# Scores ahead of the turned probabilities, in a two-block transformer kernel on one core

## The chip, the core and the metric

The kernel runs on one NeuronCore of a Trainium2 chip. TensorE (PE) multiplies matrices: a weight load puts a stationary operand into the array (PEld in the trace), a matmul streams the moving operand past it into PSUM, eight banks of 512 floats per partition. VectorE (DVE) and ScalarE (ACT) work on SBUF and PSUM, GpSimd (POOL) does a few small operations and DMA issues, SyncE (SP) issues the stream of weights. Each engine works through its own queue in order; between engines only semaphores order the work. The metric is the device time of one execution in microseconds, the median of three runs.

## The reference

Two blocks of two layers each on a sequence of 256 tokens, width 1024, float32. In the first block every layer is a half FFN, a mixing of four attention branches, and another half FFN. The four branches (MLA, sliding window, NSA and differential attention) are all softmax attention over 256 keys:

```python
s = jnp.einsum('bhqd,bhkd->bhqk', qb, k).astype(jnp.float32) * scale
s = s + rel_bias(table, qpos, kpos)[:, None]
s = jnp.where(kpos[None, :] <= qpos[:, None], s, NEG)
p = jax.nn.softmax(s, -1)
return jnp.einsum('bhqk,bhkd->bhqd', a.astype(v.dtype), v)
```

Each branch is projected and gated: `merged + sigmoid(u @ w_gate) * (y @ w_branch)`. The first layer of the second block has dilated attention: 16 heads, three groups of dilation 1, 4 and 16, a softmax in each group and one over the groups. The second layer has retention instead, which the change leaves alone.

## The kernel before

All weights come as one stream of slots (3072 floats per partition) through a ring of four. Most slots are split on the chip into a high part (ACT, L1456, `ring_hi`) and a low part (DVE, L1778, `ring_lo`), and PE multiplies high by high, high by low and low by high (`uT,ring_hi` and `uT,ring_lo` in the trace, all at L829, the helper `mm`). PE says by the semaphore `ring_used` that a slot has been read. The helper `mm` carries that signal: a finished slot adds to `pending`, and the next call of `mm` sends it. Transposes and the values of dilated attention don't go through `mm`.

**Attention of the first block.** Two heads make a pair. There are 20 pairs per layer (0 to 3 MLA, 4 to 7 sliding window, 8 to 11 differential, 12 to 19 NSA) and 22 steps. Before the change, step t does on PE, in this order:

- `turn(l, t)` (L1101): transposes of the probabilities of pair t-1, 128x128 each, six of them (three for a differential pair). It waits for `probs_normed`, which DVE signals.
- `scores(l, t)`: queries times keys of pair t into PSUM banks 0 and 1. It waits for `biased`, by which DVE says that the scores of pair t-1 have been read.
- two projections or merges (24 matmuls or more with `uT,ring_hi`), each waiting for its PSUM bank, which DVE empties (`qkT`, L2074, or `mlaT_all`, L2334).
- `values(l, t-1)`: probabilities times values for pair t-1.

DVE in step t: `bias_max` (L2256, L2258, adds the bias and takes the maximum), a low split (L1778), an addition of a branch (L2332, L2334), `normalise` (from L2272), a gate. ACT in step t: a high split (L1456), `copy_pT` (L1675, the transposed probabilities out of PSUM), a gate (L1680), then `exps` (L1663, L1664). DVE's and ACT's orders are written out and the same after the change.

The array is used in three cuts. The trace writes them as rows*columns: transposes and projections are 128*128, the scores of all pairs but MLA have a contraction of 64 and run in two halves by rows, 64*128, and the values of all pairs but differential write 64 columns each, 128*64.

**Dilated attention.** 17 steps for 16 score blocks (`NS2` = 16). Step s does `dilated_turn(s-1)` (L1295, eight transposes), `dilated_scores(s)` (12 matmuls, L829, `qkT`), four projections for the next pair of heads (`dilated_pieces`, none from step 14 on), and `dilated_values(s-1)` (L1309). DVE: `dilated`, bias and maximum at L1937, then low splits and copies of projections (L1912), then reciprocal and scaling (L1956, L1957). ACT: copies of the transposes (L1544), exps (L1549), copies of projections and high splits. At the end of an odd step ACT stands before a high split which waits for `ring_used` of the slot that the last projection of that step has read. The signal is still `pending` then, and is sent by the first matmul of the next scores.

Of the kernel before, what the change touches and what calls it, by code (L numbers as in the profile page):

```python
# [166 lines left out]
def build(nc, stream, x_rows, norm_gT_2, gains_2, table_2, pick_2, ret_const, decay, norm_gT, mla_gT, sinks, posT, lam, subln, table_1, consts, flip_dram, pick_1, out):  # L167

    ctx = ExitStack()
    with ctx:  # L170
# [276 lines left out]
        NS2 = HEADS_2  # L447
# [92 lines left out]
        PAIRS = NU // 2  # L540
# [37 lines left out]
        def unit_q(u):  # L578
            kind, n = u["kind"], u["head"]
            if kind == "mla":  # L580
                return mlaT[:, n, 0:SEQ]
            if kind == "diff":
                return qkT[64 * u["map"]:64 * u["map"] + 64, T_DQ + n, :]
            base = T_SQ if kind == "swa" else T_NQ
            return qkT[64 * (n // 4):64 * (n // 4) + 64, base + n % 4, :]

        def unit_k(u):
            kind, n = u["kind"], u["head"]
            if kind == "mla":
                return mlaT[:, n, SEQ:2 * SEQ]  # L590
            if kind == "diff":
                return qkT[64 * u["map"]:64 * u["map"] + 64, T_DK + n, :]
            tile = {"swa": T_SK, "sel": T_KS, "win": T_KW}[kind]
            return qkT[64 * (n // 4):64 * (n // 4) + 64, tile, :]
# [21 lines left out]
        def piece(l, what, n):  # L616

            return l * PIECES_LAYER + PIECE_INDEX[what, n]
# [16 lines left out]
        def piece_copied(n):  # L635

            mine = sum(ON_ACT[:n + 1])
            return (piece_act_out, mine) if ON_ACT[n] else (piece_dve_out, n + 1 - mine)
# [7 lines left out]
        def tile_at(i):  # L646

            return 9 + i if i < 12 else None

        def merge_at(i):  # L650

            return i - 12 if i >= 12 else None
# [143 lines left out]
        def _(pe):  # L796
# [31 lines left out]
            def mm(out_, lhsT, rhs, start, stop, **kw):  # L828
                m = pe.matmul(out_, lhsT, rhs, start=start, stop=stop, **kw)  # L829
                if pending[0]:  # L830
                    m.then_inc(ring_used, pending[0])
                    pending[0] = 0
                return m
# [232 lines left out]
            def scores(l, t):  # L1066
                a, two = l * NU + 2 * t, UNITS[2 * t:2 * t + 2]
                if a >= 2:
                    pe.wait_ge(biased, a)
                if t == 0:  # L1070
                    pe.wait_ge(*piece_copied(piece(l, "head", 6)))
                    pe.wait_ge(*piece_copied(piece(l, "head", 7)))
                if t in (4, 8, 12):
                    pe.wait_ge(*piece_copied(piece(l, "tile", {4: 6, 8: 20, 12: 20}[t])))
                for cols, q_cols, k_cols in ((slice(0, P), slice(0, P), slice(0, P)),
                                             (slice(P, 3 * P), slice(P, SEQ), slice(0, SEQ))):
                    for j, u in enumerate(two):
                        m = mm(ps[:, j, cols], unit_q(u)[:, q_cols], unit_k(u)[:, k_cols], True, True)
                        if cols.start:
                            m.then_inc(scores_ready, 1)  # L1080

            def turn(l, t):
                if t in (2, 3):
                    pe.wait_ge(cmp_taken, 2 * l + t - 1)
                if t == 4:
                    pe.wait_ge(cmp_kv_out, l + 1)
                if t == 5:
                    pe.wait_ge(cmp_vB, l + 1)
                if t == 6:
                    pe.wait_ge(cmp_shifted, l + 1)  # L1090
                if t == 9:
                    pe.wait_ge(cmp_pT, l + 1)
                if t == 15:
                    pe.wait_ge(branch_in, COPIES_LAYER * l + COPIES_OF_BRANCH[3])
                for j in range(jobs(t - 1)):
                    n = jobs_before(l, t - 1) + j
                    pe.wait_ge(probs_normed, n + 1)
                    if l or t > 1:
                        pe.wait_ge(pT_ready, jobs_before(l, t - 1))
                    for b in range(3):  # L1100
                        last = pe.transpose(ps[:, 2 + j, b * P:(b + 1) * P], probs_sb[:, j, b * P:(b + 1) * P], ident)  # L1101
                    last.then_inc(probs_turned, 1)
# [43 lines left out]

            def attention(l):
                for t in range(STEPS):
                    if 1 <= t <= PAIRS:
                        turn(l, t)  # L1150
                    if t < PAIRS:
                        scores(l, t)
                    for i in (2 * t, 2 * t + 1):
                        if tile_at(i) is not None:
                            tile(l, tile_at(i))
                        else:
                            merge(l, merge_at(i))
                        compress(l, t, i % 2)
                        if i == 28:
                            turn_diff(l, t)  # L1160
                    if 1 <= t <= PAIRS:
                        values(l, t - 1)
# [103 lines left out]
            def dilated_scores(s):  # L1266


                hp, qt = s // 2, s % 2
                b = hp % 2  # L1270
                if qt == 0:
                    pe.wait_ge(*piece_copied(PIECES_DIL + 8 * hp + 5))
                if s:
                    pe.wait_ge(biased_2_ready, 2 * s)
                for g in range(N_GROUPS):
                    for j in range(2):
                        r = slice(64 * j, 64 * j + 64)
                        q = qkD[r, b, 2 * g, qt * P:(qt + 1) * P]
                        k = qkD[r, b, 2 * g + 1, :] if g == 0 else qkD[r, b, 2 * g + 1, qt * P:(qt + 1) * P]
                        o = ps[:, j, 0:256] if g == 0 else ps[:, j, 128 * (g + 1):128 * (g + 2)]  # L1280
                        m = mm(o, q, k, True, True)
                        if g == N_GROUPS - 1:
                            m.then_inc(scores_2, 1)
# [30 lines left out]
            def dilated(c0, p):  # L1314
                dilated_pieces(c0, 0, range(8), p)
                for s in range(NS2 + 1):
                    if s:
                        dilated_turn(s - 1)
                    if s < NS2:
                        dilated_scores(s)  # L1320
                    hp = s // 2 + 1
                    if hp < 8:
                        dilated_pieces(c0, hp, range(4 * (s % 2), 4 * (s % 2) + 4), p)
                    if s:
                        dilated_values(s - 1)
                pe.wait_ge(pT_2_ready, 2 * NS2)
                out_project(c0 + 24, lambda k, tt: mT_2[:, k, tt * P:(tt + 1) * P], KD, p, (stored_2, 1))
# [1372 lines left out]
```

## Time and profile before

| what | value |
|---|---|
| median of three runs | 2904.51 us (2904.24 to 2905.25) |
| the profiled execution | 2901.78 us |
| its span, first to last instruction | 2900.0 us |
| PE, DVE, ACT, POOL busy | 96%, 62%, 46%, 4% |
| attention of the first block, layer 0 | about 304 to 531 us |
| attention of the first block, layer 1 | about 1047 to 1274 us |
| dilated attention | about 1747 to 1990 us |

A row of a timeline gives start and length in microseconds, the engine, the line, the operation and its operands, and in brackets how long the engine had been idle before it and who released it. A row of the waits gives engine and line, who was waited for, the sum, the number and the longest.

### The profile page before, as it was taken

Reading aid. Unit: us, or ns where it says so; the run is one execution under the profiler, and the core shown is the slowest. Engines: PE = TensorE matmul, PEld = TensorE weight load, DVE = VectorE, ACT = ScalarE, POOL = GpSimd, SP = SyncE. Lnnn points to the kernel's source line nnn. Section 1 sums busy time; section 2 is a strip of 40 time slices with the busy share of each in tenths; the row PEclk is TensorE's granted clock in tenths of the full one; section 3 lists DMA queues with packets and bytes.
Section 4 is the critical chain, followed back from the end, with each engine's and each line's share of the span. In section 5 each row is a group of like instructions: output and inputs, shape, how many; then the busy total and the mean of one; then the engine's idle time right before and its main releaser. Section 6 shows DMA issues by size and latency. Waiting matters only on the chain.

```text
span 2900.0 us, 41202 instructions
## 1 busy us (share of the span) xinstructions
PE 2798.5 (96%) x16526; PEld 2384.0 (82%) x16526; DVE 1795.7 (62%) x2753; ACT 1328.2 (46%) x1913; POOL 104.0 (4%) x135
## 2 busy tenths in 40 slices
PE   7999999999999999999999999998999998999998
PEld 6888988688888888877878879996887887986787
DVE  5666566366766656645667665554667666652665
ACT  4553444155554444424554544443545554451444
POOL 1000000000000000001002001110000000000000
PEclk9999999999999999999999999999999999999999
DMA  6554333345454543345555445443454554434443
GB/s 239 189 199 153 139 147 131 139 167 195 174 184 184 196 153 132 131 152 208 194 186 183 182 165 171 168 156 128 174 192 161 187 195 153 174 133 151 165 183 123
DMA packets 49042, 488.40 MB, mean 168 GB/s; under 512 B 6480, under 2 KB 6576, under 8 KB 10520
## 3 DMA queue, kind: packets, MB, share of 16 engines
q1 hardware_dynamic: 43192, 470.44, 44.1%
q0 software_dynamic: 5728, 16.25, 1.9%
q8 instruction: 87, 1.43, 0.2%
q14 instruction: 35, 0.29, 0.0%
HBM read 485.47 MB, written 1.19 MB: 168 GB/s over the span
## 4 chain that ended last, share of the span: by engine, by line
PE 87%; DVE 6%; ACT 3%; issue 2%; DMA 1%; POOL 0%; DVEq 0%; ACTq 0%; POOLq 0%
PE ps L829 67%; PE ps L887 16%; DVE ring_lo L1778 2%; ACT ring_hi L1456 2%; PE ps L1101 1%; PE ps L845 1%; DMA norm_g<-norm_gT_dram 1%; PE ps L1295 1%; PE ps L1309 1%; PE ps L1206 0%; DVE xn L1888 0%; DVE uT L1802 0%; PE ps L898 0%; PE ps L953 0%; DVE h L1897 0%
## 5 line engine op out<-in xcount | busy, mean ns | idle before, releaser
L829 PE MATMUL ps<-uT,ring_hi 128*128 128x512 f32 (+1 forms) x5536 | 1516.1, 345 | 30.6 <-DVE mlaT_all L2334 10.9
L829 PE MATMUL ps<-uT,ring_lo 128*128 128x256 f32 x4176 | 1176.4, 282 | 0.0
L829 PEld LDWEIGHTS ps<-uT,ring_hi 128*128 128x128 f32 x5536 | 955.4, 190 | 185.8 <-DVE ring_lo L1778 18.2
L829 PEld LDWEIGHTS ps<-uT,ring_lo 128*128 128x128 f32 x4176 | 794.4, 190 | 6.2
L1854 DVE TENSOR_TENSOR ring_lo<-ring,ring_hi 128x2048 fp32r<-128x2048 f32 x167 | 382.8, 2292 | 230.8 <-ACT ring_hi L1498 230.8
L1778 DVE TENSOR_TENSOR ring_lo<-ring,ring_hi 128x3072 fp32r<-128x3072 f32 (+1 forms) x100 | 297.0, 2971 | 172.7 <-ACT ring_hi L1456 172.6
L1456 ACT ACTIVATE ring_hi<-ring 128x3072 fp32r<-128x3072 f32 (+1 forms) x100 | 246.0, 2460 | 320.1 <-PE ps L829 227.6
L1498 ACT ACTIVATE ring_hi<-ring 128x2048 fp32r<-128x2048 f32 x174 | 330.8, 1901 | 0.0
L887 PE MATMUL ps<-ring_hi,hid_hi 128*128 128x512 f32 x704 | 276.8, 393 | 9.8 <-DVE hid_lo L1849 9.8
L887 PE MATMUL ps<-ring_lo,hid_hi 128*128 128x512 f32 x704 | 276.0, 392 | 0.0
L887 PE MATMUL ps<-ring_hi,hid_lo 128*128 128x512 f32 x704 | 274.0, 389 | 0.0
L829 PE MATMUL ps<-ring_hi,uT 128*128 128x384 f32 (+1 forms) x1024 | 258.9, 332 | 3.4 <-DVE ring_lo L1778 1.8
L1488 ACT ACTIVATE work_all<-ps 128x512 f32<-128x512 f32 x176 | 105.3, 598 | 327.3 <-PE ps L829 327.0
L1491 ACT ACTIVATE work_all<-work_all 128x256 f32<-128x256 f32 x176 | 73.7, 418 | 318.5 <-DVE work_all L1842 318.5
L1834 DVE TENSOR_TENSOR ring_lo<-ring,ring_hi 128x1024 fp32r<-128x1024 f32 x176 | 214.5, 1219 | 0.5 <-ACT ring_hi L1486 0.5
L829 PEld LDWEIGHTS ps<-ring_hi,uT 128*128 128x128 f32 x1024 | 183.5, 188 | 5.5 <-DVE ring_lo L1778 4.4
L1486 ACT ACTIVATE ring_hi<-ring 128x1024 fp32r<-128x1024 f32 x176 | 184.0, 1045 | 0.0
L829 PE MATMUL ps<-ring_lo,uT 128*128 128x384 f32 (+1 forms) x512 | 169.2, 330 | 0.0
L887 PEld LDWEIGHTS ps<-ring_hi,hid_hi 128*128 128x128 f32 x704 | 132.1, 188 | 43.9 <-DVE hid_lo L1849 13.1
L887 PEld LDWEIGHTS ps<-ring_hi,hid_lo 128*128 128x128 f32 x704 | 132.2, 188 | 29.1
L887 PEld LDWEIGHTS ps<-ring_lo,hid_hi 128*128 128x128 f32 x704 | 132.2, 188 | 21.0
L1839 DVE TENSOR_TENSOR work_all<-ps,work_all 128x512 f32<-128x512 f32 x176 | 121.4, 690 | 43.5 <-ACT work_all L1488 43.2
(274 smaller groups left out, 2493.3 us busy)
## 6 DMA issues: line engine op xcount, KB each, us to landing
ring<-stream_dram SPq DMA_DIRECT2D x299, 1536.0 KB, 6.3
mlaT_all<-bias_vectors POOLq DMA_DIRECT2D x32, 96.0 KB, 2.9
bias<-gains_dram POOLq DMA_DIRECT2D x5, 512.0 KB, 7.7
yR<-bias_vectors POOLq DMA_DIRECT2D x1, 2048.0 KB, 10.5
mlaT_all<-bias_vectors POOLq DMA_DIRECT2D x32, 64.0 KB, 3.3
row<-ret_const_dram POOLq DMA_DIRECT2D x1, 1280.0 KB, 5.8
h<-x_rows_dram POOLq DMA_DIRECT2D x2, 512.0 KB, 11.6
yR<-gains_dram POOLq DMA_DIRECT2D x2, 512.0 KB, 11.4
```

What stands on the lines that cost most here:

```text
L829: m = pe.matmul(out_, lhsT, rhs, start=start, stop=stop, **kw)
L845: last = pe.transpose(ps[:, banks[kp], j * SEQ + tt * P:j * SEQ + tt * P + P], h[:, tt, k * P:(k + 1) * P], ident)
L887: last = pe.matmul(ps[:, n, :], x, w[:, cols], start=False, stop=final and x is x_lo, skip_group_check=True)
L1456: act.activation(split_part(c, high(c)), split_part(c, ring[:, c % NS, :]), ACT.Copy)\
L1486: act.activation(high(c)[:, 2 * D:3 * D], ring[:, c % NS, 2 * D:3 * D], ACT.Copy).then_inc(down_hi, 1)
L1488: act.activation(gu_low, ps[:, 4 + 2 * (g % 2):6 + 2 * (g % 2), SEQ:2 * SEQ], ACT.Copy)\
L1491: act.activation(sil[:, g % 2, :], gu[:, g % 2, 0, :], ACT.Silu).then_inc(silu_ready, 1)
L1498: act.activation(high(c)[:, 0:2 * D], ring[:, c % NS, 0:2 * D], ACT.Copy).then_inc(hi_ready, 1)
L1778: dve.tensor_tensor(split_part(c, ring_lo[:, c % NS, :]), split_part(c, ring[:, c % NS, :]), split_part(c, high(c).bitcast(F32)), ALU.subt ...
L1834: dve.tensor_tensor(ring_lo[:, c % NS, 2 * D:3 * D], ring[:, c % NS, 2 * D:3 * D], high(c)[:, 2 * D:3 * D].bitcast(F32), ALU.subtract)
L1839: dve.tensor_tensor(gu[:, g % 2, :, :], ps[:, 4 + 2 * (g % 2):6 + 2 * (g % 2), 0:SEQ], gu_low, ALU.add).then_inc(gu_summed, 1)
L1854: dve.tensor_tensor(ring_lo[:, c % NS, 0:2 * D], ring[:, c % NS, 0:2 * D], high(c)[:, 0:2 * D].bitcast(F32), ALU.subtract).then_inc(lo_rea ...
```

## The change

In both loops the call for the scores is put in front of the call for the transposes. Nothing is added or removed, on no engine; DVE's, ACT's, POOL's and SP's orders stay as they are. A blank line that comes with it moves the line numbers behind it by one (L1295 and L1309 are L1296 and L1310 in the changed kernel).

```diff
@@ attention(l), first block @@
                 for t in range(STEPS):
+
+                    if t < PAIRS:
+                        scores(l, t)
                     if 1 <= t <= PAIRS:
                         turn(l, t)
-                    if t < PAIRS:
-                        scores(l, t)
@@ dilated(c0, p) @@
                 for s in range(NS2 + 1):
+                    if s < NS2:
+                        dilated_scores(s)
                     if s:
                         dilated_turn(s - 1)
-                    if s < NS2:
-                        dilated_scores(s)
```

PE in step 18 of the first block's attention, layer 0, before. `yR,ring` are the last matmuls of step 17's merge, `work_all,row` the values of pair 16, `cst,work_all` the transposes, `qkT` the scores, `uT` the next merge:

```order
L829 MATMUL ps<-yR,ring 128x256 x4
L829 MATMUL ps<-work_all,row 64x256 x2
L829 MATMUL ps<-work_all,row 64x128 x2
L1101 MATMUL ps<-cst,work_all 128x128 x6
L829 MATMUL ps<-qkT 128x128 x2
L829 MATMUL ps<-qkT 128x256 x2
L829 MATMUL ps<-uT,ring_hi 128x256 x2
L829 MATMUL ps<-uT,ring_lo 128x256
```

The same place in the changed kernel:

```order
L829 MATMUL ps<-yR,ring 128x256 x4
L829 MATMUL ps<-work_all,row 64x256 x2
L829 MATMUL ps<-work_all,row 64x128 x2
L829 MATMUL ps<-qkT 128x128 x2
L829 MATMUL ps<-qkT 128x256 x2
L1101 MATMUL ps<-cst,work_all 128x128 x6
L829 MATMUL ps<-uT,ring_hi 128x256 x2
L829 MATMUL ps<-uT,ring_lo 128x256
```

The six transposes have moved behind the four score matmuls, right ahead of the merge; values and scores now follow each other directly.

PE at the end of dilated attention, steps 14 to 16, before (`mlaT_all,work_all` are transposes, `work_all,row` values; the last rows are the output projection):

```order
L1309 MATMUL ps<-work_all,row 64x128 x8
L1295 MATMUL ps<-mlaT_all,work_all 128x128 x8
L829 MATMUL ps<-qkT 128x256 x2
L829 MATMUL ps<-qkT 128x128 x4
L1309 MATMUL ps<-work_all,row 64x128 x8
L1295 MATMUL ps<-mlaT_all,work_all 128x128 x8
L829 MATMUL ps<-qkT 128x256 x2
L829 MATMUL ps<-qkT 128x128 x4
L1309 MATMUL ps<-work_all,row 64x128 x8
L1295 MATMUL ps<-mlaT_all,work_all 128x128 x8
L1309 MATMUL ps<-work_all,row 64x128 x8
L829 MATMUL ps<-ring,yR 128x512 x28
```

And in the changed kernel:

```order
L1310 MATMUL ps<-work_all,row 64x128 x8
L829 MATMUL ps<-qkT 128x256 x2
L829 MATMUL ps<-qkT 128x128 x4
L1296 MATMUL ps<-mlaT_all,work_all 128x128 x8
L1310 MATMUL ps<-work_all,row 64x128 x8
L829 MATMUL ps<-qkT 128x256 x2
L829 MATMUL ps<-qkT 128x128 x4
L1296 MATMUL ps<-mlaT_all,work_all 128x128 x8
L1310 MATMUL ps<-work_all,row 64x128 x8
L1296 MATMUL ps<-mlaT_all,work_all 128x128 x8
L1310 MATMUL ps<-work_all,row 64x128 x8
L829 MATMUL ps<-ring,yR 128x512 x28
```

The last scores (second group of `qkT`) no longer stand behind the transposes of step 14's probabilities.

## Rows read from the trace of the kernel before

**Rows 1.** The page's first part: busy time, share of the span, instructions.

```profile
PE 2798.5 (96%) x16526; PEld 2384.0 (82%) x16526; DVE 1795.7 (62%) x2753; ACT 1328.2 (46%) x1913; POOL 104.0 (4%) x135
```

**Rows 2.** The page's chain that ended last, by engine.

```profile
PE 87%; DVE 6%; ACT 3%; issue 2%; DMA 1%; POOL 0%; DVEq 0%; ACTq 0%; POOLq 0%
```

**Rows 3.** PE's waits in attention, layer 0, 330 to 530 us: sum, times, longest.

```profile
PE ps L829 <- DVE mlaT_all L2334: 5.4, 4, 2.7
```

**Rows 4.** PE's waits in attention, layer 1, 1070 to 1271 us.

```profile
PE ps L829 <- DVE mlaT_all L2334: 5.5, 5, 2.7
```

**Rows 5.** PE's waits in dilated attention, 1720 to 1992 us.

```profile
PE ps L829 <- DVE qkT L1912: 4.0, 7, 2.0
PE ps L1295 <- DVE work_all L1957: 3.6, 4, 1.6
```

**Rows 6.** Timeline of PE, step 18 of layer 0: transposes, scores, merge.

```profile
502.18 0.87 PE L1101 MATMUL ps<-cst,work_all 128*128 128x128 f32 x6
502.99 0.93 PE L829 MATMUL ps<-qkT 64*128 64x128 f32 x8
503.84 0.50 PE L829 MATMUL ps<-uT,ring_hi 128*128 128x256 f32 x2
504.18 0.28 PE L829 MATMUL ps<-uT,ring_lo 128*128 128x256 f32 x1
504.30 0.40 PE L829 MATMUL ps<-uT,ring_hi 128*128 128x256 f32 x2
```

**Rows 7.** Timeline of PE, step 10 of layer 0 (differential, values uncut): transposes, scores.

```profile
407.09 0.49 PE L1101 MATMUL ps<-cst,work_all 128*128 128x128 f32 x3
407.51 0.93 PE L829 MATMUL ps<-qkT 64*128 64x128 f32 x8
```

**Rows 8.** Timeline of all engines, step 18 of layer 0.

```profile
502.12 2.77 ACT L1456 ACTIVATE ring_hi<-ring 128x3072 fp32r<-128x3072 f32 x1 [3.47 <-PE ps L829]
503.94 0.29 DVE L2256 CUSTOM_DVE_ANT_0 xn<-ps,bias 128x128 f32<-128x128 f32 x1 [2.03 <-PE ps L829]
505.50 3.35 DVE L1778 TENSOR_TENSOR ring_lo<-ring,ring_hi 128x3072 fp32r<-128x3072 f32 x1
509.69 0.50 PE L829 MATMUL ps<-uT,ring_hi 128*128 128x256 f32 x2 [0.99 <-DVE mlaT_all L2334]
```

**Rows 9.** Timeline of all engines, step 2 of dilated attention, an even step.

```profile
1779.83 1.09 PE L1295 MATMUL ps<-mlaT_all,work_all 128*128 128x128 f32 x8
1780.85 1.15 PE L829 MATMUL ps<-qkT 64*128 64x256 f32 x12
1781.64 2.77 ACT L1456 ACTIVATE ring_hi<-ring 128x3072 fp32r<-128x3072 f32 x1 [2.15 <-PE ps L829]
1784.45 3.36 DVE L1778 TENSOR_TENSOR ring_lo<-ring,ring_hi 128x3072 fp32r<-128x3072 f32 x1 [0.54 <-ACT ring_hi L1456]
1787.67 0.28 PE L829 MATMUL ps<-uT,ring_lo 128*128 128x256 f32 x1
1788.29 0.48 PE L829 MATMUL ps<-uT,ring_hi 128*128 128x256 f32 x2 [0.34 <-DVE qkT L1912]
```

**Rows 10.** Timeline of all engines, steps 15 and 16 of dilated attention.

```profile
1981.44 0.65 PE L1295 MATMUL ps<-mlaT_all,work_all 128*128 128x128 f32 x4 [1.62 <-DVE work_all L1957]
1982.91 1.15 PE L829 MATMUL ps<-qkT 64*128 64x256 f32 x12
1983.02 0.60 ACT L1544 ACTIVATE work_all<-ps 128x512 f32<-128x512 f32 x1 [0.29 <-PE ps L1295]
1984.09 0.69 DVE L1937 CUSTOM_DVE_ANT_1 xn<-ps,mlaT_all 128x512 f32<-128x512 f32 x1 [1.82 <-PE ps L829]
1985.02 0.72 ACT L1549 ACTIVATE work_all<-xn,small 128x512 f32<-128x512 f32 x1 [1.40 <-DVE small L1941]
1988.81 1.98 PE L1309 MATMUL ps<-work_all,row 128*64 128x128 f32 x16 [0.69 <-ACT work_all L1544]
```

**Rows 11.** Window: length; busy PE, PEld, DVE, ACT, POOL; granted clock; DMA.

```profile
1988.50:1994.80 6.30, 6.00 (x21) 3.41 (x22) 1.06 (x6) 4.17 (x6) 0.00 (x0) 0.50 0.00 0
```

## The prediction

> **What bounds the kernel now.** I read the page first: PE is busy for 2798.5 of 2900.0 us [rows 1], and the chain that ended last runs over PE for 87% of the span [rows 2]. So the time is PE's own pace plus the few stretches in which it waits. DVE at 62% and ACT at 46% matter only where they release PE. The reader should see from this that a change of order can pay in two ways alone: PE's instructions follow each other faster, or a wait of PE gets shorter.
>
> Next came PE's waits in the three stretches that the change touches. Attention of the first block has 5.4 us in layer 0 and 5.5 us in layer 1, all on DVE's addition of a branch [rows 3, 4]. None stands on L1101: the transposes never wait there, and the scores don't either. Dilated attention has 4.0 us on DVE's copy of a projection, seven times, and 3.6 us in front of its transposes, four times [rows 5]. Those are all the waits that can be won. Last I read the timelines to see what holds these waits, and how PE gets from one kind of matmul to the next.
>
> **Part 1: fewer changes of the array's cut.** The same transposes take 1.09 us for eight [rows 9] and 0.65 us for four [rows 10], each with a change of cut ahead of it, so one more transpose is 0.44 / 4 = 0.11 us. In step 10, where the values ahead are uncut and the transposes follow without a change, three last 0.42 us from their start to the scores' start [rows 7], against 3 x 0.11 = 0.33: 0.09 us go at the change to 64*128. In step 18 six last 502.99 - 502.18 = 0.81 us against 0.66 [rows 6]: 0.15, so a group behind a change also loses some 0.06 on its second instruction. Behind the scores, the merge's first two matmuls take 0.34 us where two at the later pitch of 0.12 (504.18 to 504.30) would take 0.24 [rows 6]: 0.10 more. A change from scores to projections thus costs 0.09 + 0.10, about 0.2 us.
>
> Now count. With values cut 128*64 ahead (as in the last of rows 10), a step before goes values, transposes, scores, projection: 128*64, 128*128, 64*128, 128*128, three changes. After it goes values, scores, transposes, projection: 128*64, 64*128, 128*128, 128*128, two changes, because transposes and projections share a cut. The one into the projection goes: 0.2 us. The other two stay, with an order that the trace doesn't have (narrow values straight into row-cut scores). I take it at the price of the others; it could be free (0.2 us better) or cost two changes (0.2 us worse, and the gain is nil).
>
> In the first block these are steps 4 to 9 and 14 to 19, since values at the end of step t-1 are those of pair t-2. MLA steps 2 and 3 keep one change (their scores are uncut) and gain nothing. Steps 10 to 13 have uncut values ahead, two changes before and two after, and win only 0.10 - 0.06, say 0.05. Steps 14, 18 and 19 end in a wait of PE on DVE that swallows what PE gains in front of it, and step 13 runs into the first of them, so none of the four counts here. That leaves 9 steps x 0.2 + 3 x 0.05 = 1.95 us per layer, 3.9 for two. Dilated attention: steps 2 to 13, 12 x 0.2 = 2.4; from step 14 on there are no projections behind. Part 1 is 6.3 us. Its bounds are 0 and, with the direct change free in the same 30 steps, 12.3.
>
> The Trainium skill, "TensorEngine Tiling (Array Packing)", Key Properties, says of the direct change, which no row shows: "Changing tiling mode (not just tile) drains the TensorE". By it narrow values into row-cut scores is one drain like the others, and part 1 would be the 6.3 us; it gives no price, so this decides nothing above.
>
> **Part 2: steps 18 and 19 of the first block.** PE waits 0.99 us at 509.69 [rows 8], and the longest wait is 2.7 us, in each layer [rows 3, 4]; that one is the same place in step 19. The chain: scores end, DVE takes bias and maximum at 503.94 (it had been idle for 2.03 us waiting for PE), then a low split of 3.35 us at 505.50, then the addition that frees PE's bank. In the new order the scores begin where the transposes began, 0.81 us sooner [rows 6], and so does DVE at 503.94. But the low split also needs ACT's high split, which ends at 502.12 + 2.77 = 504.89 [rows 8] and hangs on the values, not on the scores. So the low split starts at about 504.95 rather than 505.50: 0.55 us. PE's wait falls from 0.99 to about 0.45 and stays a wait, so the whole 0.55 is won. Four such places (two steps, two layers): 2.2 us. Bounds 0 and 4 x 0.81 = 3.2.
>
> What do the moved transposes hold up? `copy_pT` stands ahead of the exps on ACT. In step 18 ACT is busy with the high split until 504.89 anyway, and the new transposes are done by then (502.18 + 0.85 for the scores + 0.81). So it costs nothing there.
>
> **Part 3: even steps of dilated attention.** Here the signal is what counts. ACT's high split at 1781.64 had been waiting for PE: for `ring_used`, pending since the end of the step before, and sent by the first score matmul, which starts at 1780.85 [rows 9]. In the new order that matmul starts where the transposes did, at 1779.83: 1.02 us sooner. ACT then starts at 1780.62, ends at 1783.39; DVE's bias and maximum come 1.02 sooner too, so its low split starts at about 1783.45 rather than 1784.45 and the copy of the projection behind it is 1.0 us earlier. PE waited for that copy: 1788.29 - 1787.67 = 0.62 against a pitch of 0.12, so 0.50 us lost [rows 9]. PE arrives 0.2 us sooner (part 1), the copy 1.0: the wait is gone with 0.3 to spare. The seven waits of rows 5 sum to 4.0; the longest, 2.0, is at step 0, which has no transposes and doesn't change. Six remain, 0.34 each in that view, 0.50 by the starts: 3.0 us. Bounds 0 and 6 x 0.62 = 3.7.
>
> **Part 4: the tail.** In steps 14 to 16 nothing covers the softmax. Before, PE does the transposes of step 14 (1981.44, and four more behind), then scores 15 at 1982.91; DVE's maximum starts at 1984.09, the exp at 1985.02 [rows 10]. In the new order scores 15 run right behind values 13, inside PE's wait of 1.62 us, so bias and maximum of 15 follow DVE's scaling of 14 at once. What is late next is ACT: its copies of step 14's transposes stand ahead of the exp and end at 1983.02 + 0.60 = 1983.62. The exp then starts at 1983.62 rather than 1985.02: 1.4 us, and all behind it, up to the last values at 1988.81, comes that much sooner. If the exps of step 14 also start sooner, it is up to 0.4 more. Bounds 0.3 (half the maximum hidden, transposes late) and 1.8.
>
> **Sum.** 6.3 + 2.2 + 3.0 + 1.4 = 12.9 us. The profiled execution took 2901.78 us, so it would be 2888.9. The median is 2904.51, 2.7 above that execution, and I take the saving off the median: 2891.6 us. Bounds of the four together: 0.3 and 21, neither end likely.
>
> **The rivals.**
> - *Waits go, changes of cut don't* (chance 0.16). Narrow values into row-cut scores costs two changes. For it: the trace has no such pair. Against it: every change that it has costs about the same. Then part 1 is nil, 6.6 us are won, 2897.9.
> - *The half-speed stretch behind the tail goes as well* (0.12). From 1988.50 to 1994.80 the granted clock was 0.50, the 1.2 GHz level, [rows 11], after PE had waited in front of the transposes of steps 15 and 16 [rows 5, 10]. In the new order those waits are shorter. At 2.4 GHz the same 6.3 us are worth 3.15: 2888.4. Against it: waits of over a microsecond remain in front of the last transposes. The Trainium skill, "TensorE: Matmul & The Clock Gate", HAM oscillation, says that gaps of the array bring the lower clock back; by it this rival is right if the rest of the gaps is short enough, which the rows before don't tell. The opposite, one more such stretch elsewhere, costs the same.
> - *Only faster following, no wait shortened* (0.06). DVE's and ACT's starts depend on something else than the scores and the signal. Against it: both were idle and released by PE [rows 8, 9]. Part 1 alone: 2898.2.
> - *Slower: the direct change is dear* (0.03). Values in column halves followed by scores in row halves occur 38 times in the new order (12 steps x 2 layers, 14 in dilated attention). If PE let the one finish wholly before it loads for the other, at 0.9 us each (as long as the scores' 0.85 us block in rows 6) instead of 0.2, it is 26.6 us lost against 12.9 won: 2918. It turns slower from 0.54 us each on. Nothing in the trace comes near this without a wait.
>
> That the change does nothing isn't a rival: PE's order moves in every step.
>
> **How the numbers follow.** My forecast has 0.60, the rivals 0.37, and 0.03 is for what I don't see. From no change this kernel's measurement can tell about 0.2%, 5.8 us. Forecast, the second and nearly all of the first and third rival are faster than that. Of the first rival (6.6) and the third (6.3) a third could fall within it, with a little from others: same 0.08. Slower 0.04, faster 0.88. The range goes from 2885 (direct change partly free, or a half-speed stretch gone) to 2898 (the first and third rival).
>
> **What would show each step.** Part 1: in step 4 to 9 the projection's first two matmuls take 0.24 us rather than 0.34, with no gap between transposes and projection. Part 2: PE's waits on L2334 about 1.1 us less per layer, so 4.3 and 4.4. Part 3: waits on L1912 once, not seven times. Part 4: scores 15 ahead of the transposes of step 14, and from those transposes' start (1981.44 before) to the last values' (1988.81) about 6 us rather than 7.4. I am wrong if PE starts to wait for the transposes' input in steps with projections, if ACT's copies of the transposes delay the exps beyond where they began before, or if dilated attention and the first block's attention together are not 10 us shorter.

## The result, and the profile after

The changed kernel takes 2884.89 us (median of four runs, 2883.84 to 2888.06) against 2904.38 us before (four runs, 2902.84 to 2905.25). The ratio is 0.9935, 95% interval 0.9918 to 0.9953: 19 us less, 14 to 24 by the interval. The forecast was 2891.6 us, 2885 to 2898. A second set of runs of the same kernel (experiment 9) gave 20 us. So the direction held, nearly all its mechanisms did, and the size was a third too small: the time lies at the lower end of the range (2884.89 against 2885), and 3 us of what brought it there were not in the forecast (see the clock below). The profiled executions give 2900.0 us of span before and 2882.4 after, 17.6 us, and that difference can be divided.

The page after, busy time and the chain by engine, to set beside [rows 1, 2]. PE is busy for 12 us less with as many instructions; that this comes from fewer changes of cut and less time at the lower clock is likely, but no run separates it. The other engines differ by 2 us at most:

```profile
PE 2786.3 (97%) x16526; PEld 2383.4 (83%) x16526; DVE 1796.6 (62%) x2753; ACT 1326.4 (46%) x1913; POOL 103.9 (4%) x135
PE 89%; DVE 5%; ACT 3%; issue 2%; DMA 1%; POOL 0%; DVEq 0%; ACTq 0%; POOLq 0%
```

PE's waits after, first block, layer 0 (330 to 530 us); layer 1 has 4.6 too. Before it was 5.4 and 5.5 [rows 3, 4]. The first row is the loader's, whose waits the prediction left out:

```profile
PEld ps L829 <- DVE mlaT_all L2335: 6.0, 5, 2.6
PE ps L829 <- DVE mlaT_all L2335: 4.6, 4, 2.3
```

PE's waits after, dilated attention (1715 to 1980 us). The copy of a projection is waited for once, not seven times, and the 3.6 us in front of the transposes [rows 5] have become 0.2. In their place stand 2.3 us in front of the values, where it was 0.7:

```profile
PE ps L1310 <- ACT work_all L1545: 2.3, 3, 0.8
PE ps L829 <- DVE qkT L1913: 2.0, 1, 2.0
PE ps L1296 <- DVE work_all L1958: 0.2, 1, 0.2
```

Step 18 of layer 0 after, PE; it answers to [rows 6]. Values, scores, transposes, merge. From the start of the first group behind the values to the third matmul of the merge it was 504.18 - 502.18 = 2.00 us, and is 501.11 - 499.30 = 1.81:

```profile
498.50 0.87 PE L829 MATMUL ps<-work_all,row 128*64 128x256 f32 x8
499.30 0.93 PE L829 MATMUL ps<-qkT 64*128 64x128 f32 x8
500.16 0.87 PE L1101 MATMUL ps<-cst,work_all 128*128 128x128 f32 x6
500.79 0.48 PE L829 MATMUL ps<-uT,ring_hi 128*128 128x256 f32 x2
501.11 0.28 PE L829 MATMUL ps<-uT,ring_lo 128*128 128x256 f32 x1
506.25 0.51 PE L829 MATMUL ps<-uT,ring_hi 128*128 128x256 f32 x2 [0.62 <-DVE mlaT_all L2335]
```

ACT and DVE in the same step, to set beside [rows 8]. The high split ends at 499.25 + 2.77 = 502.02, and the low split starts at 502.05: DVE no longer holds it up, ACT does. Its idle time in front of the maximum fell from 2.03 to 1.23 us:

```profile
499.25 2.77 ACT L1457 ACTIVATE ring_hi<-ring 128x3072 fp32r<-128x3072 f32 x1 [3.90 <-PE ps L829]
500.26 0.29 DVE L2257 CUSTOM_DVE_ANT_0 xn<-ps,bias 128x128 f32<-128x128 f32 x1 [1.23 <-PE ps L829]
502.05 3.36 DVE L1779 TENSOR_TENSOR ring_lo<-ring,ring_hi 128x3072 fp32r<-128x3072 f32 x1
505.77 0.43 DVE L2335 TENSOR_TENSOR mlaT_all<-mlaT_all,work_all 128x256 f32<-128x256 f32 x1
```

Step 2 of dilated attention after, to set beside [rows 9]. The high split starts 0.80 us behind the first score matmul, as before (1781.64 - 1780.85 = 0.79), but the scores now come first, so ACT's idle time is 1.13 instead of 2.15 us. The row before the last is the matmul that had waited 0.34 us; it follows the one at 1779.86 by 0.12:

```profile
1772.22 1.15 PE L829 MATMUL ps<-qkT 64*128 64x256 f32 x12
1773.02 2.78 ACT L1457 ACTIVATE ring_hi<-ring 128x3072 fp32r<-128x3072 f32 x1 [1.13 <-PE ps L829]
1773.30 1.09 PE L1296 MATMUL ps<-mlaT_all,work_all 128*128 128x128 f32 x8
1775.83 3.36 DVE L1779 TENSOR_TENSOR ring_lo<-ring,ring_hi 128x3072 fp32r<-128x3072 f32 x1 [0.55 <-ACT ring_hi L1457]
1779.10 0.42 DVE L1913 SCALAR_TENSOR_TENSOR qkT<-ps,r_row 128x256 f32<-128x256 f32 x1
1779.86 0.28 PE L829 MATMUL ps<-uT,ring_lo 128*128 128x256 f32 x1
1779.98 0.40 PE L829 MATMUL ps<-uT,ring_hi 128*128 128x256 f32 x2
1780.22 0.28 PE L829 MATMUL ps<-uT,ring_lo 128*128 128x256 f32 x1
```

The tail after, to set beside [rows 10]: scores 15 stand in PE's old wait, the eight transposes of step 14 run in one piece, ACT copies both halves in one piece and goes on to the exp. From those transposes to the last values it is 1973.49 - 1968.19 = 5.30 us; it was 1988.81 - 1981.44 = 7.37:

```profile
1967.12 1.15 PE L829 MATMUL ps<-qkT 64*128 64x256 f32 x12
1968.19 1.09 PE L1296 MATMUL ps<-mlaT_all,work_all 128*128 128x128 f32 x8
1968.29 0.69 DVE L1938 CUSTOM_DVE_ANT_1 xn<-ps,mlaT_all 128x512 f32<-128x512 f32 x1
1968.88 1.08 ACT L1545 ACTIVATE work_all<-ps 128x512 f32<-128x512 f32 x2 [1.45 <-PE ps L1296]
1969.86 0.72 ACT L1550 ACTIVATE work_all<-xn,small 128x512 f32<-128x512 f32 x1
1973.49 1.10 PE L1310 MATMUL ps<-work_all,row 128*64 128x128 f32 x16 [0.69 <-ACT work_all L1545]
```

The window of 6.30 us from the last values on, columns as in [rows 11], starting 0.3 us later in the work, at the values themselves. Before, the clock there was 0.50 and PE got through 21 matmuls; now it is 1.00, the 2.4 GHz level, and 29:

```profile
1973.49:1979.79 6.30, 6.30 (x29) 3.26 (x30) 2.21 (x7) 3.93 (x5) 0.00 (x0) 1.00 0.00 0
```

**Where the time went.** PE has the same matmuls in both kernels, so each can be matched with itself. The table gives how far PE's starts moved against the profile before, as differences over a stretch (minus is gained). Half-speed stretches that differ between the two stand in rows of their own.

| stretch | forecast | after |
|---|---|---|
| first block, layer 0 | -3.05 | -3.9 |
| first block, layer 1 | -3.05 | -4.1 |
| dilated attention, steps 2 to 13 | -5.4 | -5.8 |
| its tail, to the last values | -1.4 | -1.9 |
| the half-speed stretch behind the tail is gone | 0 | -3.0 |
| other half-speed stretches, start | 0 | +1.1 |
| sum | -12.9 | -17.6 |

So 15.7 us come from the order of the instructions. The rest is nearly all where PE ran at the lower clock: a stretch at 1517 us got shorter (-1.3), the one at 1715 cost 0.4 more, and one each appeared at 1749 and 2005 (+1.5, +0.8).

### The profile page after: what moved, and what is told of

The parts are those of the page before. It is cut to its first block, busy times and chain, and to the rows that moved or that the text cites. A ratio compares the mean times of both kernels' runs of the same rounds, so it can differ in the third digit from the quotient of the medians.

```text
span 2882.4 us, 41202 instructions
## 1 busy us (share of the span) xinstructions
PE 2786.3 (97%) x16526; PEld 2383.4 (83%) x16526; DVE 1796.6 (62%) x2753; ACT 1326.4 (46%) x1913; POOL 103.9 (4%) x135
## 4 chain that ended last, share of the span: by engine, by line
PE 89%; DVE 5%; ACT 3%; issue 2%; DMA 1%; POOL 0%; DVEq 0%; ACTq 0%; POOLq 0%
PE ps L829 68%; PE ps L887 16%; ACT ring_hi L1457 2%; DVE ring_lo L1779 1%; PE ps L845 1%; PE ps L1101 1%; DMA norm_g<-norm_gT_dram 1%; PE ps L1296 1%; PE ps L1310 1%; PE ps L1207 0%; DVE xn L1889 0%; DVE uT L1803 0%; PE ps L898 0%; PE ps L953 0%; PE ps L857 0%
```

## Experiments

Nine runs were made, the last of them the changed kernel again. All times are medians with the runs' range; the kernel before took 2902.92 us (2900.44 to 2905.26, 15 runs) beside experiments 1 to 4, 2903.26 (2900.3 to 2905.12, 15 runs) beside 5, 6 and 9, and 2903.03 (2900.31 to 2906.09, 19 runs) beside 7 and 8.

### 1. The new order in the first block alone

```diff
 attention(l), kernel before
-                    if 1 <= t <= PAIRS:
-                        turn(l, t)
                     if t < PAIRS:
                         scores(l, t)
+                    if 1 <= t <= PAIRS:
+                        turn(l, t)
```

> The kernel before with the scores moved ahead of the transposes in the first block's attention alone. Theory (the parts add up, each at its own place): PE's instructions there come 8.0 us sooner, as between the two kernels' traces: per layer 12 steps with narrow values ahead win 0.2 us each (less where a wait swallows it), steps 18 and 19 win 0.35 to 0.4 us more each on DVE's chain, and steps 11 to 13, 16 and 17 win 0.1 to 0.4 us more each where DVE's addition held the loader for 0.2 us. Dilated attention from its first scores to the output projection is as long as before (PE's waits there 4.0 us on L1912 and 3.6 us on L1295). Time: about 2904.4 - 8 = 2896.4 us, plus or minus 3 for where the half-speed stretches fall. Rival (most of the gain is in clock stretches that went away by the change as a whole): PE's instructions before any half-speed stretch win less than 4 us.

Measured: 2895.99 us (2893.74 to 2897.44, 8 runs), ratio 0.9975, 0.9964 to 0.9986, so 7.3 us (4 to 10). PE's starts gained 3.9 us in layer 0, 4.1 in layer 1, and nothing in dilated attention (-7.52 before its steps, -7.54 behind them). The profile's waits, layer 0:

```profile
PE ps L829 <- DVE mlaT_all L2334: 4.6, 4, 2.4
```

They are those of the changed kernel, and dilated attention has those of before, 4.0 and 3.6 us. The two swaps are independent, and the first block is worth 8, not 6 us.

### 2. The new order in dilated attention alone

```diff
 dilated(c0, p), kernel before
-                    if s:
-                        dilated_turn(s - 1)
                     if s < NS2:
                         dilated_scores(s)
+                    if s:
+                        dilated_turn(s - 1)
```

> The kernel before with the scores moved ahead in dilated attention alone. Theory: the first block's attention as before (5.4 and 5.5 us of PE's waits on the addition); from the transposes of step 1 of dilated attention to those of step 14 PE gains 6.1 us (12 x 0.2 from fewer changes of cut, 6 x 0.57 from the wait on L1912, the rest 0.3), the tail up to the last values 1.4 to 1.8 us. Time: about 2904.4 - 8 = 2896.4 us, plus or minus 3 for the half-speed stretches. Rival (the gain in dilated attention came because PE arrives there at another phase of the weights' stream, by the gain in the first block): less than 3 us there.

Measured: 2893.83 us (2891.01 to 2896.4, 8 runs), ratio 0.9967, 0.9957 to 0.9978: 9.6 us (6 to 12). PE's starts gained 5.8 us in steps 2 to 13, 1.9 in the tail, and again about 3 behind it, where the granted clock is 1.00 as in the changed kernel. With experiment 1 that is 16.9 us by the ratios, against 19 to 20 for both at once, within the intervals.

### 3. The signal alone

Old order, but the slot's signal goes with the first transpose of a step instead of waiting for the first score matmul.

```diff
 dilated_turn(s), kernel before
                     for n in range(4):
                         last = pe.transpose(ps[:, 2 + j, n * P:(n + 1) * P], ...)
+                        if pending[0]:
+                            last.then_inc(ring_used, pending[0])
+                            pending[0] = 0
```

> The kernel before, its order unchanged; only the signal that a slot has been read is sent by the first transpose of dilated attention's step instead of the first score matmul behind them. Theory (the signal held the chain): ACT's high split in even steps starts 1.02 us sooner, DVE's low split then waits for bias and maximum only and starts 0.55 us sooner, and the wait of PE on L1912 falls from 0.34 to nothing in steps 2 to 12: one wait of 2.0 us stays of 4.0 us, and PE gains about 3.0 to 3.4 us there; the three changes of cut stay at their price. Rival (what counted was that the scores, and so DVE's maximum, came sooner): the low split starts where it did, the seven waits stay and nothing is won.

Measured: 2898.75 us, from one run, so the reading rests on the profile and not on the time. PE's waits in dilated attention:

```profile
PE ps L1295 <- DVE work_all L1960: 3.6, 4, 1.6
PE ps L829 <- DVE qkT L1915: 2.0, 1, 2.0
```

The six waits on the copy are gone and the four in front of the transposes stay. PE's starts gain 0.56 us in each of six even steps and nothing in the odd ones: 3.4 us. Together with 0.2 us in each of twelve steps this is 5.8, the whole of what the changed kernel gains there. So in the even steps it is the signal that counts, and one can have it without the new order. In the tail nothing moved.

### 4. The low split behind the addition, steps 18 and 19

The changed kernel, with DVE's addition of a branch (which frees PE's bank) ahead of the low split in two steps.

```diff
-        LATE_SPLITS = (0, 2)
+        LATE_SPLITS = (0, 2, 18, 19)
```

> The changed kernel with the splits of steps 18 and 19 of the first block's attention moved behind the exps on ACT and behind the scaling of the probabilities on DVE, as steps 0 and 2 have them. Theory (the 3.36 us low split stands between DVE's maximum and the addition that PE waits for): PE's waits on L2335 fall from 0.6 and 2.3 us per layer to nearly nothing in front of the first merge; the split is late by about 3 us and must be back before the next step's merges, some 7 us later. PE gains up to 5 us in both layers, time about 2880 us. Rival (the late split holds DVE's gate for the second merge, whose bank PE needs in the next step, or ACT's split comes after the exps and frees the ring later): waits move to L2316's release and the gain is under 2 us, or a loss.

Measured: 2881.02 us (2878.0 to 2882.82, 4 runs), ratio 0.9921, 0.9904 to 0.9937. PE's waits, layer 0, then the row of the new one, in step 20:

```profile
PE ps L829 <- DVE gate_in L2316: 1.7, 1, 1.7
PE ps L829 <- DVE mlaT_all L2335: 1.7, 2, 0.9
```

```profile
520.75 0.50 PE L829 MATMUL ps<-uT,ring_hi 128*128 128x256 f32 x2 [1.72 <-DVE gate_in L2316]
```

DVE's low split:

```profile
505.34 3.36 DVE L1779 TENSOR_TENSOR ring_lo<-ring,ring_hi 128x3072 fp32r<-128x3072 f32 x1 [1.24 <-ACT ring_hi L1457]
```

Two waits are gone: step 18 gains 1.45 us against the kernel before, where the changed kernel gains 0.56. But both splits are now late (this high split starts at 502.55 instead of 499.25), and PE meets 1.7 us of it again in step 20, at a gate that DVE computes behind the low split. In layer 1, where no half-speed stretch interferes, steps 18 to 20 gain 1.4 + 3.2 - 2.0 = 2.6 us against the kernel before, and the changed kernel gains 1.1 there: 1.5 us per layer more, not the 2.5 that were hoped for. In time the two can't be told apart, since the intervals of their ratios overlap. The split's order does set PE's waits, and ACT's place in the chain counts as much as DVE's.

### 5. The scores between the two heads' transposes

The kernel before, first block; three transposes of head 1, the scores, three of head 2. DVE gets its scores half as early as in the changed kernel, but the number of changes of the array's cut is that of before.

```diff
 attention(l), kernel before
                     if 1 <= t <= PAIRS:
-                        turn(l, t)
+                        turn(l, t, range(1))
                     if t < PAIRS:
                         scores(l, t)
+                    if 1 <= t <= PAIRS:
+                        turn(l, t, range(1, 2))
```

> The kernel before with the scores of the first block's attention between the transposes of the pair's first head and those of its second (values, three transposes, scores, three transposes, projection); differential pairs, with three transposes in all, and dilated attention stay as before. Theory (each change of the array's cut has its price, 0.15 us into transposes, 0.2 us into scores or a projection): there are three changes again, into transposes, scores and transposes, 0.50 us against 0.55, so steps 4 to 9 win 0.05 us each and not 0.2. Steps 18 and 19 win 0.33 us each, since the scores come three transposes sooner. In all about 2 us less in PE's instructions of the two layers, 2902 us or so with the half-speed stretches. Rival (what pays is that the transposes, which wait for nothing, stand next to the projection and cover its semaphores): steps 4 to 9 win 0.2 us each as in the changed kernel.

Measured: 2900.09 us (2898.22 to 2901.41, 10 runs), ratio 0.9989, 0.998 to 0.9998. PE in step 18, layer 0:

```profile
500.08 0.55 PE L1103 MATMUL ps<-cst,work_all 128*128 128x128 f32 x3
500.56 0.93 PE L829 MATMUL ps<-qkT 64*128 64x128 f32 x8
501.42 0.55 PE L1103 MATMUL ps<-cst,work_all 128*128 128x128 f32 x3
501.72 0.48 PE L829 MATMUL ps<-uT,ring_hi 128*128 128x256 f32 x2
502.04 0.28 PE L829 MATMUL ps<-uT,ring_lo 128*128 128x256 f32 x1
```

From 500.08 to 502.04 it is 1.96 us: 2.00 before, 1.81 after the change. What a step gains, layer 0, from PE's starts at the end of each step, in us:

| step | between heads | changed kernel |
|---|---|---|
| 6 to 8, each | 0.04 | 0.20 |
| 10 | 0 | 0.05 |
| 11, 12 | 0 | 0.23, 0.22 |
| 13 | 0.13 | 0.13 |
| 14 | 0 | 0.01 |
| 15 | 0.04 | 0.20 |
| 16, 17 | 0.22 each | 0.38 each |
| 18 | 0.32 | 0.56 |

In the steps without a wait (6 to 8, 15) nearly all of the 0.2 needs one change of cut less; 0.04 come with as many changes as before, in another order. Steps 16 and 17 show a second part, 0.18, that comes without it. In steps 9 to 12 the pair has one job of three transposes, so this kernel's order is that of before, and nothing moves; the changed kernel gains 0.19 in step 9.

### 6. Gate and addition ahead of the splits, steps 15 to 19

The changed kernel; ACT does the gate before its high split, DVE the addition before its low split.

```diff
 attention(l) on ACT, changed kernel
+                    if 15 <= t < 20:
+                        gate(l, merge_at(2 * t - 1))
                     if t in SPLIT_STEPS and t not in LATE_SPLITS:
                         take_high(mix_slot(l) + SPLIT_STEPS[t])
 attention(l) on DVE, changed kernel
+                    if 15 <= t < 20:
+                        add(2 * t - 1)
                     if t in SPLIT_STEPS and t not in LATE_SPLITS:
                         take_low(mix_slot(l) + SPLIT_STEPS[t])
                     ... (the old places of both skip these steps)
```

> The changed kernel, and in steps 15 to 19 of the first block's attention ACT takes the gate of the step's first merge ahead of its high split, and DVE the addition of that branch ahead of its low split; the splits stay where they start otherwise. Theory (PE waits in steps 18 and 19 because the addition that empties its bank stands behind the 3.36 us low split; moving the split to the end of the step only moved the wait, since DVE idled 1.2 us for ACT's split and the gate of the second merge came late): the waits of 0.6 and 2.3 us on L2335 per layer go, and no wait on L2316 takes their place, since DVE idles less. 3 us per layer, 6 in all, against the changed kernel of the same call: about 2879 us where that one has 2885. Rival (DVE is full in these steps and any order ends in the same place, as its low split has to be done for the next step): the wait comes back at step 20 on L2316 at 1.5 us or more, and the gain is under 3 us in all.

Measured: 2877.14 us (2875.62 to 2877.78, 4 runs), ratio 0.9906, 0.9891 to 0.9922: the fastest kernel here, 6.6 us below the changed kernel in the same set, as expected. PE's waits in layer 1:

```profile
PE ps L829 <- DVE mlaT_all L2337: 1.7, 2, 0.9
```

Only those of step 14 are left. ACT and DVE in step 18 show the two things that experiment 4 lacked: the high split starts where the gate ends, and the low split is on time (501.94, against 505.34 there):

```profile
498.40 0.42 ACT L1681 ACTIVATE gate_out<-gate_in 128x256 f32<-128x256 f32 x1 [3.73 <-DVE gate_in L2318]
498.72 2.75 ACT L1457 ACTIVATE ring_hi<-ring 128x3072 fp32r<-128x3072 f32 x1
```

```profile
501.59 0.42 DVE L2337 TENSOR_TENSOR mlaT_all<-mlaT_all,work_all 128x256 f32<-128x256 f32 x1
501.94 3.35 DVE L1781 TENSOR_TENSOR ring_lo<-ring,ring_hi 128x3072 fp32r<-128x3072 f32 x1
```

### 7. The new order in steps 14 and 15 of dilated attention alone

```diff
 dilated(c0, p), kernel before
+                    if s < NS2 and s >= 14:
+                        dilated_scores(s)
                     if s:
                         dilated_turn(s - 1)
-                    if s < NS2:
+                    if s < NS2 and not s >= 14:
                         dilated_scores(s)
```

> The kernel before with the new order only in steps 14 and 15 of dilated attention. Theory (the tail's gain stands by itself, and shorter waits in it keep the half-speed stretch behind it away): PE's starts move by nothing before step 14, by 1.9 us (1.7 to 2.1) from there to the last values, and the window of 6.30 us from the last values' start shows a granted clock of 1.00, so about 3 us more: 4.9 us in all behind the output projection, 2898 us. Rival A (the half-speed stretch depends on the whole of dilated attention, on its even steps' waits, not on the tail's): 1.9 us, the window still at 0.50 to 0.76, 2901 us. Rival B (the stretches fall by chance): either, and it doesn't go with the order.

Measured: 2899.91 us (2897.65 to 2901.53, 10 runs), ratio 0.9987, 0.9978 to 0.9997. Before step 14 PE's starts don't move (+0.36 at its start, +0.34 behind step 13), behind the tail they have gained 4.9 us: 1.9 in the tail, 3.0 in the window after it, whose clock is 1.00:

```profile
1987.27:1993.57 6.30, 6.30 (x29) 3.26 (x30) 2.22 (x7) 3.92 (x5) 0.00 (x0) 1.00 0.00 0
```

This is what the theory expected. By the medians the time is only 3.1 us shorter. In this profile 1.0 us is lost again at a half-speed stretch at 2019 us and 2.0 us at one at 2695; whether that holds for the other nine runs, no profile shows.

### 8. The new order in dilated attention up to step 13 alone

The same edit with the condition the other way round (`s < 14`), on the kernel before. The expectation calls it the changed kernel; what ran has the old order in the first block as well. So it stands beside experiment 2, from which it differs by the tail alone, and its total can't be held against the times expected.

> The changed kernel with the old order in steps 14 and 15 of dilated attention. Theory: PE's waits in the tail are those of before (1.62, 1.52 and 0.69 us), 1.9 us are given back, and with those waits the half-speed stretch is back in the window of 6.30 us from the last values' start (granted clock 0.50 to 0.76), so 3.4 to 4.9 us are given back against the changed kernel: 2887 to 2889 us. Rival A (the even steps of dilated attention decide on the stretch): 1.9 us given back, the window at 1.00, 2886 us. Rival B (chance): no connection with the order.

Measured: 2895.68 us (2894.93 to 2896.98, 10 runs), ratio 0.9977, 0.9967 to 0.9987, so 1.9 us behind experiment 2. PE's starts gain 5.8 us in steps 2 to 13 and 0.0 in the tail. PE's waits in the tail are those of before, and yet the window behind it shows the full clock:

```profile
1977.35 0.65 PE L1295 MATMUL ps<-mlaT_all,work_all 128*128 128x128 f32 x4 [1.62 <-DVE work_all L1959]
1982.51 0.66 PE L1295 MATMUL ps<-mlaT_all,work_all 128*128 128x128 f32 x4 [1.52 <-DVE work_all L1959]
1984.71 1.09 PE L1309 MATMUL ps<-work_all,row 128*64 128x128 f32 x16 [0.69 <-ACT work_all L1546]
```

```profile
1984.71:1991.01 6.30, 6.30 (x29) 3.26 (x30) 2.21 (x7) 3.92 (x5) 0.00 (x0) 1.00 0.00 0
```

The theory of experiment 7, that shorter waits in the tail keep the lower clock away, falls with this.

### 9. The changed kernel again

> The changed kernel as it is, once more, for a tighter interval and a second profile. Theory (15.6 us come from the order of PE's instructions, the rest from where half-speed stretches fell in one execution): PE's instructions win the same 4.0, 4.1, 5.8 and 1.9 us in the two layers' attention, in dilated attention up to the last scores, and in the tail, wherever the half-speed stretches lie; the ratio to before is 0.9946 give or take 0.001. Rival (the stretches that went are part of the effect): the ratio is 0.9935 or less again, and the new profile lacks the 6.8 us at half speed behind dilated attention too.

Measured: 2883.76 us (2883.47 to 2887.37, 5 runs), ratio 0.9931, 0.9918 to 0.9945. Dilated attention gains 5.8 us again and its tail 1.9, and the window behind it shows 1.00 again, with 3.0 us more: what the expectation's rival says. Elsewhere this profile has more half-speed stretches than the first one (at 1047, 1259, 2423 and 2686 us, for example), and its span is 3.2 us longer.

## Why the prediction fell short

**Fewer changes of the cut (6.3 us): right, and its price too.** Steps 4 to 9 gained 0.18 to 0.21 us each, step 10 gained 0.05, the odd steps of dilated attention 0.2. Experiment 5 shows that the number of changes pays, since the transposes' split around the scores brings 0.04. The direct change from values to row-cut scores, of which no row told, costs what the others do: from values to the next group it is 499.30 - 498.50 = 0.80 us after, as in experiment 5 (500.08 - 499.28). The rival that makes it cost two is out, and the dear one too. Only the place of the 0.2 us was wrong. I had put half of it in the projection's first two matmuls, which should have fallen from 0.34 to 0.24 us; they take 0.32 (501.11 - 500.79). It lies nearly all at the boundary: six transposes with scores behind them take 0.81 us [rows 6], with the merge behind them 500.79 - 500.16 = 0.63.

**Steps 18 and 19 (2.2 us): the mechanism was right, and the 0.55 us too.** The low split started when ACT's high split ended, as forecast. Step 18 gained 0.56 in all. The sign that was to show it was miscounted: PE comes to the wait 0.2 us sooner, so a gain of 0.56 takes only 0.99 - 0.62 = 0.37 off the wait, and the waits of a layer fell to 4.6 us, not to 4.3.

**The mis-sized term was the count of waits in the first block.** "Steps 14, 18 and 19 end in a wait of PE" and no other step did, by the four waits of [rows 3]. But the loader waits too. In the profile before it has nine such waits in layer 0, and five of them stand before the second merge of a step, like this one of step 11:

```profile
PEld ps L829 <- DVE mlaT_all L2334: 8.2, 9, 2.9
424.42 0.30 PEld L829 LDWEIGHTS ps<-uT,ring_hi 128*128 128x128 f32 x2 [0.32 <-DVE mlaT_all L2334]
```

In the changed kernel that place has no wait (row of the same instruction):

```profile
422.77 0.59 PE L829 MATMUL ps<-uT,ring_hi 128*128 128x256 f32 x2
```

The matmul that was streaming covers the loader's wait but for some 0.18 us, so PE's own row shows no idle time. Scores that come sooner bring DVE's addition sooner there too. It is 0.18 us in steps 11, 12, 16 and 17. Step 13, which the forecast counted as nothing, gained 0.13; there the loader's wait only fell from 0.32 to 0.24. That is 0.85 us per layer, 1.7 in both, and 0.2 us more in step 17 of layer 1: the difference between 6.1 and 8.0 us. Experiment 1 shows it with nothing else changed, and steps 16 and 17 of experiment 5 show it apart from the cut.

**The signal (3.0 us): right, 3.4 measured.** Experiment 3 isolates it. Each wait was worth 0.56 rather than 0.50 us, because the second matmul behind this stall was late as well: from the one that waited, at 1788.29 [rows 9], to the third it took 0.31 us, against 1780.22 - 1779.98 = 0.24 after. The row before, behind the stall:

```profile
1788.60 0.28 PE L829 MATMUL ps<-uT,ring_lo 128*128 128x256 f32 x1
```

**The tail (1.4 us): right, 1.9 measured.** I let the exp wait for ACT's second copy at its old end, 1983.62. But the eight transposes now run without the pause between the halves, and ACT does both copies in 1.08 us. Counted from the transposes' start, the exp came 1969.86 - 1968.19 = 1.67 us behind; before it was 1985.02 - 1981.44 = 3.58.

**The clock.** The rival with the half-speed stretch came true on top of the forecast: 3.0 us, more than any other part of the miss. The prediction gave it a chance of 0.12 and left it out of the sum. Its place was right and its reason wasn't. What the prediction held against it was wrong too: no wait of over a microsecond remained in the tail. The longest left is 0.8 us, in front of the values, and the one in front of the last transposes is 0.2. The window is at the full clock in all six kernels with any part of the new order in dilated attention, including experiment 8, where the waits before it are as long as ever. It is at half speed, in whole or in part, in the four others: before 0.50, experiment 3 0.51, experiment 5 0.50, and experiment 1, whose row this is, 0.76:

```profile
1981.26:1987.56 6.30, 6.30 (x25) 3.63 (x26) 1.34 (x7) 3.92 (x5) 0.00 (x0) 0.76 0.00 0
```

Experiment 3 shortens the waits of the even steps and keeps the stretch. The Trainium skill, "TensorE: Matmul & The Clock Gate", HAM oscillation, has the lower clock follow gaps of the array. Here the same gaps of 1.62, 1.52 and 0.69 us come with a clock of 0.50 in the kernel before and of 1.00 in experiment 8, so these gaps alone don't decide it. Nor is the lower clock simply gone. In all seven profiles with a part of the new order in dilated attention, and in experiment 1, another, shorter half-speed stretch stands some 31 to 34 us behind the last values' start, at a cost of 0.6 to 1.2 us; before, experiment 3 and experiment 5 have none there (1.00 from 2018 to 2026 us before). In the changed kernel it is the one at 2005 us, which the table counts among the others:

```profile
2003.00:2009.00 6.00, 3.86 (x20) 3.77 (x21) 5.24 (x11) 2.68 (x7) 0.54 (x1) 0.72 0.40 115
```

So at this place of the kernel some 2 us are won by the clock, and not 3. These are eleven profiles, one of each kernel and two of the changed one, in which other such stretches move from one to the next. That the 3 us go with the new order is what they agree on; it is not shown to be caused by it, and why the stretch goes, or moves, is open.

Between the two profiles the miss is 17.6 - 12.9 = 4.7 us: 2.8 us of sizes (1.9 in the first block, 0.4, 0.5), 3.0 for that stretch, less 1.1 for the others. By the medians it is 2 us more, which one profile of each doesn't show.

## What to carry to other kernels

Put matmuls that cut the array the same way next to each other; here a change saved was worth 0.2 us, and how many are saved could be counted from the order alone. When asking which waits of PE an earlier release can shorten, read the loader's waits as well as PE's: a wait of 0.32 us hid there behind the matmul that was still streaming, and cost 0.18. Look for what an instruction carries besides its work: in the even steps the gain came from a semaphore that rode on the first score matmul, and a three-line edit got it without any new order.

## What the runs showed of the hardware

Transposes of float32 and matmuls of the split operands, both uncut, follow each other with no pause: the merge's first matmul starts 0.03 us behind the last of the transposes, where the scores start 0.20 us behind it (single matmuls of step 6, layer 0, after and before). From the last start of one group to the first of the next it is 0.20 us from values to transposes, 0.20 from values to scores and 0.20 from transposes to scores, and 0.31 from scores to transposes or to the merge; two transposes follow each other at 0.11. A stretch at half speed (granted clock 0.50) disappears or comes with edits that leave the work around it as it was, and costs up to 3 us at a place; two kernels that differ by 2 or 3 us in time can't be told apart by one profile each.
